# A new order for the work of a mixer stage: forget gate beside the latents, value rows under the attention, levels between gate pieces, gate bounds made in the block before

## What is computed

```python
h = h + 0.5 * (silu(n1(h) @ w1_gate) * (n1(h) @ w1_up)) @ w1_down          # phase 6
u = rms_norm(h, ln_mix) @ w_in                                            # phase 7
hq, hf, hi, hg, cq, ckv, kr = split(u, [512, 512, 512, 512, 256, 128, 64])
lb = cumsum(softmax(hg_lb_logits, axis=0))[0]         # the gate bounds
log_f = log(lb + (1 - lb) * sigmoid(hf));  k_in = (1 - lb) * sigmoid(-hf)
o_hg = gated_recurrence(hq, log_f, k_in, hi)          # in chunks of 64, 4 heads
o_hg = rms_norm(o_hg, hg_out_norm) * silu(hg)
q = rms_norm(cq) @ w_q_up;  kv = rms_norm(ckv) @ w_kv_up     # 4 heads, 128 + 64 rotated
o_mla = causal_softmax_attention(rope(q), rope(k, kr), v)
h = h + concat(o_hg, o_mla) @ w_out
```

## Time and profile before

| | us |
|---|---|
| median of 3 runs | 1299.99 (1299.95 to 1301.54) |
| the profiled execution's own time | 1299.59 |
| its span in the trace | 1297.8 |
| PE busy | 1231.9 (95%) |
| DVE, ACT, POOL busy | 931.2, 639.5, 123.1 |
| granted clock of PE over the span | 0.986 |

### The profile page before, as it was taken

One profiled execution on the slowest core, in us unless ns is written; L12 is line 12 of the kernel. 1 busy time (PEld: TensorE's weight loads), 2 busy tenths in 40 slices (PEclk: granted clock), 3 DMA queues, 4 the chain that ended last, 5 costly groups with the idle time before them and its releaser, 6 DMA issues. The chain is left out here.

```text
span 1297.8 us, 17412 instructions
## 1 busy us (share of the span) xinstructions
PE 1231.9 (95%) x6886; PEld 1056.2 (81%) x6886; DVE 931.2 (72%) x1108; ACT 639.5 (49%) x914; POOL 123.1 (9%) x246
## 2 busy tenths in 40 slices
PE   6999899999999989999999999999789789999997
PEld 5889788888779977888887888888668678888885
DVE  6656688788876778987778766665747967666666
ACT  5555544444666664444447544443546444444444
POOL 3000310000120001000003000000115410000002
PEclk8999999999999999999999999999899899999999
DMA  9644275555355335655554455553333335555550
GB/s 271 185 144 130 82 252 194 195 195 194 101 176 195 105 123 170 229 183 182 183 180 171 160 197 194 195 190 134 121 123 130 98 98 175 182 184 179 184 191 33
DMA packets 149012, 214.49 MB, mean 165 GB/s; under 512 B 4410, under 2 KB 114428, under 8 KB 148932
## 3 DMA queue, kind: packets, MB, share of 16 engines
q1 hardware_dynamic: 145756, 205.65, 47.6%
q0 software_dynamic: 1632, 4.71, 1.4%
q10 hardware_dynamic: 1544, 3.02, 0.7%
HBM read 212.30 MB, written 1.06 MB: 164 GB/s over the span
## 5 line engine op out<-in xcount | busy, mean ns | idle before, releaser
L1059 DVE TENSOR_TENSOR w_lo<-raw,w_hi 128x2048 fp32r<-128x2048 f32 (+1 forms) x195 | 444.2, 2287 | 29.2 <-ACT w_hi L611 29.1
L2049 PE MATMUL work<-hT_both,w_hi 128*128 128x512 f32 x1280 | 455.1, 398 | 0.0
L611 ACT ACTIVATE w_hi<-raw 128x2048 fp32r<-128x2048 f32 (+1 forms) x195 | 368.1, 1894 | 4.5 <-DMA raw<-in_na_w_qkv 2.4
L2051 PE MATMUL work<-hT_both,w_lo 128*128 128x256 f32 x1280 | 359.1, 281 | 0.0
L2049 PEld LDWEIGHTS work<-hT_both,w_hi 128*128 128x128 f32 x1280 | 240.5, 188 | 58.6
L2051 PEld LDWEIGHTS work<-hT_both,w_lo 128*128 128x128 f32 x1280 | 241.7, 189 | 3.0
L1653 PE MATMUL acc<-w_hi,aux_hi 128*128 128x512 f32 x384 | 151.5, 394 | 3.0 <-DVE aux_lo L1449 3.0
L1654 PE MATMUL acc<-w_lo,aux_hi 128*128 128x512 f32 x384 | 150.4, 392 | 0.0
L1655 PE MATMUL acc<-w_hi,aux_lo 128*128 128x512 f32 x384 | 149.6, 390 | 0.0
L1423 DVE TENSOR_REDUCE Z<-work 128x256 f32<-128x512 f32 x88 | 60.5, 687 | 96.6 <-PE work L2051 87.6
L899 ACT ACTIVATE aux_hi<-Z 128x256 fp32r<-128x256 f32 x88 | 36.8, 419 | 133.7 <-DVE Z L1445 133.7
(11 more groups left out here) (232 smaller groups left out, 1819.7 us busy)
## 6 DMA issues: line engine op xcount, KB each, us to landing
raw<-in_ffn_w_in SPq DMA_DIRECT2D x44, 1024.0 KB, 5.9
raw<-in_ffn_w_out SPq DMA_DIRECT2D x22, 1024.0 KB, 5.0
raw<-in_w_gate SPq DMA_DIRECT2D x22, 1024.0 KB, 5.5
raw<-in_w_up SPq DMA_DIRECT2D x22, 1024.0 KB, 6.0
raw<-in_w_down SPq DMA_DIRECT2D x22, 1024.0 KB, 5.0
raw<-in_na_w_qkv SPq DMA_DIRECT2D x12, 1024.0 KB, 7.5
raw<-in_da_w_qkv SPq DMA_DIRECT2D x12, 1024.0 KB, 5.6
raw<-in_ple_w_gate SPq DMA_DIRECT2D x8, 1024.0 KB, 5.1
```

The costliest lines, as they stand in the source:

```text
L611: act.activation(w_hi[:, n % RING, 0:size], raw[:, n % RAW, 0:size], ACT.Copy).then_inc(hi_done, 1)
L1059: dve.tensor_tensor(w_lo[:, n % RING, 0:size], raw[:, n % RAW, 0:size], w_hi[:, n % RING, 0:size].bitcast(F32), ALU.subtract).then_inc(lo_ ...
L2049: pe.matmul(b.rearrange("p (e s) -> p e s", e=2), v[0][:, k, cols(c % 2)], hT_both[:, k, :, :], start=k == 0, stop=False)
L2051: ins = pe.matmul(b[:, 0:S], v[1][:, k, cols(c % 2)], hT_hi[:, k, :], start=False, stop=k == KT - 1)
```

## The change

- The forget gate's slabs now stand second in the mixer's list. PE's order is c0, hf0, c1, hf1, m, the first half of hq, q, kn, vm, the second half of hq, qt (4 groups in place of 5: rotated parts are packed), cum, kt.
- The value rows `hi` stand around the first scores, and one gate piece and level 0 stand between the transpose of a head's weights and its product with the values. The other gate pieces and the first piece of the output product stand between levels.
- The attention output's transpose stands before level 1. The gate sum is copied out of `acc` and gets its Silu later.
- Gate bounds are made in phase 6, in three portions on DVE (`bounds`), with the exponential on ACT after tile 5.
- POOL's masks and differences follow the running sum, so they lie beside the attention.
- Buffers move within `Z` to make room.

The core of the diff, with PE's list in full:

```diff
 # plan
-            stage("attm", 2 * MLA_HEADS)
...
+            for u in range(MLA_HEADS):
+                stage(f"T7.{u}", 1)
+                if u == MLA_HEADS - 1:
+                    stage("lev0", 2)
+                stage(f"V7.{u}", 1)
             stage("omla", 2, 2)
 # ACT, phase 6
+                    if ph == 6 and c == 5:
+                        act.wait_ge(lb_max, 1)
+                        act.activation(lbr, lbr, ACT.Exp).then_inc(lb_exp, 1)
 # ACT, mixer
+                feed(b + 13)
+                decay(0)
+                exps7(0)
+                exps7(1)
+                feed(b + 14)
+                for t in range(T):
+                    evac(G["hi"] + t, hv[:, t, :], bank(G["hi"] + t))
+                weights_turned7(0)
+                weights_turned7(1)
+                exps7(2)
+                exps7(3)
+                weights_turned7(2)
+                decay(1)
+                weights_turned7(3)
+                feed(b + 15)
+                decay(2)
 # DVE, phase 6 (called after tile c)
+            def bounds(c):
+                if c == 4:
+                    dve.wait_ge(lb_loaded, 16)
+                    link(dve.tensor_tensor(lbt, lbr[:, 0, :], lbr[:, 1, :], ALU.max))
+                    dve.tensor_tensor(lbr[:, 0, :], lbr[:, 0, :], lbt, ALU.subtract)
+                    dve.tensor_tensor(lbr[:, 1, :], lbr[:, 1, :], lbt, ALU.subtract).then_inc(lb_max, 1)
+                if c == 7:
+                    dve.wait_ge(lb_exp, 1)
+                    link(dve.tensor_tensor(lbt, lbr[:, 0, :], lbr[:, 1, :], ALU.add))
+                    link(dve.reciprocal(lbt, lbt))
+                if c == 9:
+                    dve.tensor_tensor(lbr[:, 0, :], lbr[:, 0, :], lbt, ALU.mult)
+                    link(dve.tensor_tensor(lbr[:, 1, :], lbr[:, 1, :], lbt, ALU.mult))
 # DVE, mixer
+                feed(b + 14)
+                scores7(2)
+                output7(0)
+                scores7(3)
+                output7(1)
+                feed(b + 15)
+                output7(2)
+                output7(3)
+                keyed(1)
+                dve.wait_ge(mask_ready, 1)
+                dve.wait_ge(a_cleared, 1)
+                gather(0)
 # PE, mixer
+                latents(0, 0)
+                turn_x(7, 1)
+                latents(0, 1)
+                forget(0, 0)
+                forget(0, 1)
+                latents(1, 0)
+                latents(1, 1)
+                forget(1, 0)
+                forget(1, 1)
                 for t in range(T):
                     evacuated(pe, G[f"c{t}"])
                     turn(G["m"] + t, [cn[:, t, cols(i)] for i in range(3)])
+                columns(G["hq0"], b + 4)
                 pe.wait_ge(part_ready, H["m"])
...
+                columns(G["hq1"], b + 7)
...
+                values(0, 0)
+                values(1, 0)
...
+                scores(0)
+                scores(1)
+                values(0, 1)
+                values(1, 1)
...
+                weights(0)
+                scores(2)
+                outputs(0)
+                weights(1)
+                scores(3)
+                outputs(1)
+                weights(2)
+                gate_piece(0, 0)
+                outputs(2)
+                weights(3)
+                level(0)
+                outputs(3)
+                gate_piece(1, 0)
+                evacuated(pe, G["V7.3"])
+                for t in range(T):
+                    turn(G["omla"] + t, [xn[:, t, cols(4 + i)] for i in range(4)])
+                level(1)
+                gate_piece(0, 1)
+                level(2)
+                gate_piece(1, 1)
+                level(3)
+                late_piece(0, 0)
+                level(4)
+                level(5)
+                level(6)
+                level(7)
...
+                late_piece(0, 1)
+                late_piece(1, 0)
+                pe.wait_ge(xn_ready, X["hg.0"])
+                turn(G["om"], [xn[:, 0, cols(i)] for i in range(4)])
+                late_piece(1, 1)
+                pe.wait_ge(xn_ready, X["hg.1"])
+                turn(G["om"] + 1, [xn[:, 1, cols(i)] for i in range(4)])
```

More of the change, by code:

```diff
@@ L928, in mixer, with latents @@
             def mixer(b):
-                for t in range(T):
+                def latents(t):
                     g = G[f"c{t}"]
-                    feed(b + 4)
                     full(act, g)
@@ L1452, in ffn @@
                         feed(b + 3 * j + 5)
+                    if ph == 6:
+                        bounds(c)
                 nb = b + 3 * STEPS
@@ new lines, in mixer @@
+                feed(b + 4)
+                tile_parts(7, 1)
+                latents(0)
+                feed(b + 5)
+                forget(0)
+                latents(1)
+                feed(b + 7)
+                turned([(G["m"] + t, aux_hi[:, 0:3, t * P:(t + 1) * P], aux_lo[:, 0:3, t * P:(t + 1) * P])
+                        for t in range(T)], G_QA)
+                forget(1)
+                feed(b + 9)
+                rope()
+                feed(b + 12)
+                for i in range(2):
+                    evacuated(dve, G["kt"] + i)
@@ L2104, in mixer, with tile_rows @@
             def mixer(b):
-                row_phase(7, lambda t: [G[f"c{t}"]], b, QLORA + KVLORA + ROPE)
+                def tile_rows(g, n, width, t, kh):
+                    pe.wait_ge(part_ready, H[f"n7.{t}"] - 1 + kh)
+                    v = slab(n + kh)
+                    d = open_bank(pe, g) if kh == 0 else work[:, g % WORK, :]
+                    for k in range(4):
+                        ins = product3(d[:, 0:width], both(hT, every, 4 * kh + k, cols(t)), both(v, every, k, every),
+                                       kh == 0 and k == 0, kh == 1 and k == 3)
+                    if kh == 1:
+                        ins.then_inc(bank_full[g % WORK], 1)
+                    elif t == 1:
+                        ins.then_inc(used, 1)
@@ new lines, in mixer, with late_piece @@
+                n = B["wo7"]
+                def late_piece(t, half):
+                    if t == 0 and half == 0:
+                        pe.wait_ge(part_ready, H["omla"])
+                        pe.wait_ge(gate_read, T)
+                        pe.wait_ge(s_free, units_before[7] + MLA_HEADS)
+                    v = slab(n + half)
+                    for k in range(4):
+                        ins = product3(acc[:, 2 * t + half, :], both(aux, every, k, cols(t)), both(v, every, k, every),
+                                       k == 0, False)
+                    if t == 1:
+                        ins.then_inc(used, 1)
```

505 lines of the change are left out of this document (249 added, 256 removed).

## The result

The changed kernel takes 1287.76 us, the median of four executions (1286.19 to 1291.37), against 1299.97 (1296.70 to 1301.54). The ratio is 0.9913, 95% interval [0.9885, 0.9942], so it is faster by 0.6 to 1.15%.

The account below looks back on a forecast made before the run. PE was taken as the bound, with time to gain only where it idles (18.0 us in 14 mixer waits) or is slowed. Gains of 19.5 less 7.0 us gave 12.5 us less, forecast 1287.2 us; 8-in-10 range 1283.5 to 1292.0.

Parts of the forecast that it names:

- A: Latents to q: three waits for DVE's scaling and splitting go, covered by hf1 and half of hq; gain 4.7 us.
- B: q, k and v products: granted clock no longer lowered after those waits, 7.0 us for 9.9; gain 2.8 us.
- C: Attention: four waits for ACT's readouts go behind scores, a gate piece or level 0; gain 4.1 us.
- D: Levels: of six waits totalling 7.3 us, all but the 3.61 before level 6 go; gain 3.5 us.
- E: The gated half's turn: its wait goes, now behind a piece of 2.8 us; gain 1.7 us.
- F and G: Mixer: four transposes fewer, 0.5 us; overlap regained at 13 waits, 0.17 us each, 2.2 us.
- The last head: Added before head 3's product with the values: wait 4.0 us, overlap 0.2, lowered clock behind it 2.8; cost 7.0 us.
- Phase 6, transfers, masks: Gate bounds in phase 6, earlier forget slabs and POOL's masks beside the attention: each predicted to cost 0.
- Rival 1: Clock stays up after the last head's wait, or that wait is shorter; 1284.4 us, chance 0.13.
- 2: Phase 6: gate bounds are not hidden; half of DVE's 7.7 us would make 1291.0 us, chance 0.12.
- 3: Attention: masks stretch DVE's work, costing 1.7 us; 1288.9 us, or 1291.7 with a clock loss; chance 0.15.
- rivals 4 and 5: Masks stretch DVE enough to be slower, 1303 us, chance 0.05; as many waits come elsewhere, 1300, chance 0.03.

Follow-up runs that it names:

- the filled kernel: Changed kernel plus 13 dummy products of 384 columns on PE between level 0 and head 3's product with the values; 1292.09 us, ratio 0.9936 to the kernel before.
- POOL quiet: Changed kernel, but POOL waits for head 2's output before clearing A and starting level 2's difference; 1290.72 us, ratio 0.9926 to the kernel before.
- in the second: Second set: the changed kernel itself again, nothing altered, six executions; 1289.22 us, ratio 0.9929 to the kernel before.
- three edits: Changed kernel with slab b + 14's split behind gather(2), b + 15's beside b + 16's, and the gated half's turns served one after the other; 1274.87 us, ratio 0.9821.
- the last kernel: Three edits plus two dummy products of 384 columns in PE's 1.90 us waits ahead of the second tile's columns in both gated blocks; 1273.71 us, ratio 0.9802.

## Why the prediction was right, step by step

The sum was 12.5 us less, of which the mixer's two traces show 12.3 and 11.3. By its terms, in the traces of after:

- **A, 4.7 us.** All three waits are gone. Right. That hq0 covers the one before q is shown by taking it away; that hf1 covers the two before the turn was not tested by itself.
- **B, 2.8 us.** The q, k and v products take 7.0 us for 9.9, 2.9 less. Right; without the cover one wait of 2.75 us brings the clock back down and costs 1.9 of it.
- **C, 4.1 us.** The four waits (4.3 us) are gone; 4.5 us of waits come back without the products between the heads.
- **D, 3.5 us.** 7.3 us in six waits became 3.95 in two, 3.4 us; the 3.60 before level 6 stayed as said. Without the products between the levels, 4.9 us of waits come back.
- **E, 1.7 us.** Wrong: 1.44 of 1.74 us are still there. I had taken a piece of 2.8 us behind the first turn for cover, and overlooked that DVE's list reads the second turn before it finishes the first part. No product ahead of the second turn can cover that, since it delays the second turn too; the order on DVE did it.
- **F and G, 2.7 us.** 11 waits went and not 13, so G is 1.9 by its own rate. F and the rate itself were not measured by themselves.
- **Not in the sum.** Levels 6 and 7 took 5.46 and 5.44 us for the 6.69, 1.2 us less, at a granted clock of 0.68 for 0.54 from level 6 to the cross product, behind the same wait. I had put this at nothing, so that it made good most of the error in E is luck. Nor is it shown to be the change's doing: the kernel before has one trace, and of eleven traces with the new order and this wait nine took 5.2 to 5.5 us, but the filled kernel took 6.31, and with POOL quiet, where this part of the list is that of the changed kernel, it was as long as before:

```profile
1020.67 6.79 PE L2218 MATMUL work<-Z 128*128 128x128 f32 x32 [3.60 <-DVE Z L1560]
```

- **The last head, 7.0 us.** The wait is 4.85 where I took 4.0 and had 4.4 as the upper end: the split took 3.25 us, and I had bounded it by 2.95. The other 0.15 us lie in the small steps of the chain; with a split of 2.29 us the wait was 3.90 where my chain gives 3.7. The clock took 2.1 to 2.3 us for my 2.8. That the two still come to 7.0 us is luck: 6.93 us was got back by moving the split.
- **Phase 6, transfers, masks, 0.** Phase 6 takes 184.4 us with and without the bounds; no wait of PE ends on a transfer; the masks are worth 0.02 us.

With the measured sizes, and F and the rate of G as I had taken them: 4.7 + 2.9 + 4.3 + 3.4 + 0.3 + 0.5 + 1.9 + 1.2 = 19.2, less 4.85 + 0.17 + 2.1 = 7.1, gives 12.1 us for the mixer. Without the unforeseen 1.2 it is 10.9. The time gained 12.2 us in the first set and 10.0 in the second. The forecast was right in its mechanism and its largest terms, and lucky in the smaller ones, whose errors cancelled.

Rival 1 (the clock stays up) is out in both traces, 2 and 3 by the experiments, 4 with 3, and 5 because only one wait was added. By the prediction's own numbers rivals 4 and 5 come to 1303.7 and 1301.2 us, not 1303 and 1300, which changes no chance.

## What to carry to other kernels

When a queue is reordered, walk the list of each engine that stands between two steps of the waited chain, and ask of each entry when its result is wanted: here one weight split, wanted 50 us later, cost 7 us, and a line moved on DVE's list was worth more than half of what the whole reordering gained. A helper that serves two jobs in a software pipeline can make the first wait for the second's input (1.4 us here); where PE waits for the first, call it once for each. Price a wait on PE with the clock behind it (here 2.1 us behind 4.85, 1.9 behind 2.75), and measure the clock by filling the wait, with a filler no longer than the wait.

## What was not expected of the hardware

The same instructions behind the same wait do not always get the same clock. Two traces of one program, the changed kernel, had 0.50 and 0.60 in the latents' first 2 us. Behind a wait of 1.90 us that ended on the same instruction, the first 2 us of the last gated block had in the first trace of the changed kernel

```profile
1067.94:1069.94 2.00, 2.00 (x12) 2.00 (x13) 0.66 (x1) 0.00 (x0) 0.00 (x0) 0.68 0.75 254
1069.94:1071.94 2.00, 2.00 (x11) 2.00 (x11) 0.80 (x2) 0.08 (x1) 0.00 (x0) 0.50 0.05 16
```

and with three edits, where this code is the same

```profile
1052.92:1054.92 2.00, 2.00 (x17) 2.00 (x18) 0.65 (x1) 0.00 (x0) 0.00 (x0) 1.00 0.72 266
```

Over 14 traces (the filled one among them) the block takes one of two lengths, 189.6 us (six) or 191.1 (eight), and nothing between. Levels 6 and 7, behind 3.60 us in twelve traces, took 5.2 to 5.5 us in most, but 6.3, 6.7 and 6.8 in three, the one of the kernel before among them. The products of the latents, behind 1.80 us of waiting, met a clock of 1.00 in one trace (POOL quiet) and about 0.5 to 0.6 in most. Everything ahead of phase 6's second tile, where PE's code is the same in all but the last kernel, took from 725.3 to 729.6 us. A few such places could make the spread of 4 to 8 us between executions of one kernel; that they do is not shown, since only one execution of each kernel was traced, two of the changed one. Either way an edit worth 1 us is read from its stretch in the trace and not from the medians. What decides between the two lengths is open; in phase 6 the lower clock went away when PE's idle time was cut from 1.90 to 0.60 us.
